# Hybrid decoder step on one core: a mixer stage with new weight slots, a packed step-size projection and a re-ordered chunk schedule

## What is computed

```python
proj = rmsnorm(x, g) @ w_in          # -> z 512 | xBC 1024 | dt 8 | q 512 | k 128 | v 128
xbc  = silu(causal_conv(xBC, width 4))
dt   = softplus(dt + dt_bias)        # step sizes, one per head
y_ssd = gated_norm(ssd_scan(xbc, dt, a, chunks of 128) + d_skip * x, z)   # 8 heads x 64, state 128
y_att = sliding_window_attention(q, k, v, window 128, sinks)              # 8 q heads, 2 kv heads
x = x + rmsnorm(concat(y_ssd, y_att) @ w_out)
mem_k, mem_v = rmsnorm(mem) @ w_xk, rmsnorm(mem) @ w_xv   # 256 rows, 1024 x 1024 each
... cross-attention into mem_k / mem_v, then a SwiGLU feed-forward
```

## Time and profile before

| what | value |
|---|---|
| median of 3 runs | 1830.93 us (1830.87 to 1839.26) |
| the profiled execution, its own time | 1835.19 us |
| its span, first to last instruction | 1833.5 us |
| busy share of the span: PE, weight loads, DVE, ACT, POOL | 91%, 86%, 49%, 41%, 12% |
| mean granted TensorE clock | 0.959 of 2.4 GHz |
| HBM traffic | 227.82 MB, 124 GB/s over the span |

### The profile page before, as it was taken

One profiled execution on the slowest core, in us unless ns is written; L12 is line 12 of the kernel. 1 busy time (PEld: TensorE's weight loads), 2 busy tenths in 40 slices (PEclk: granted clock), 3 DMA queues, 4 the chain that ended last, 5 costly groups with the idle time before them and its releaser, 6 DMA issues. The chain is left out here.

```text
span 1833.5 us, 27884 instructions
## 1 busy us (share of the span) xinstructions
PE 1675.7 (91%) x10764; PEld 1582.9 (86%) x10764; DVE 899.8 (49%) x1162; ACT 755.5 (41%) x1375; POOL 216.2 (12%) x317
## 2 busy tenths in 40 slices
PE   6999989778675998999999999999999999999996
PEld 6988777667654998999988999999999999999996
DVE  3466777766443365533444544443354443355443
ACT  3455655554333344443334433333233333344432
POOL 1012222222200012122222000000000000000000
PEclk9999999899975999999999999999999999999998
DMA  6542333222333854344353534454344453355651
GB/s 173 127 115 73 70 104 81 58 78 72 113 100 111 208 138 141 104 133 155 116 172 116 161 116 129 124 148 126 104 138 127 125 154 114 110 159 174 174 173 58
DMA packets 394147, 227.82 MB, mean 124 GB/s; under 512 B 33972, under 2 KB 384288, under 8 KB 394035
## 3 DMA queue, kind: packets, MB, share of 16 engines
q1 hardware_dynamic: 389442, 209.73, 40.1%
q0 software_dynamic: 4608, 16.78, 2.6%
HBM read 217.42 MB, written 10.07 MB: 124 GB/s over the span
## 5 line engine op out<-in xcount | busy, mean ns | idle before, releaser
L2547 DVE TENSOR_TENSOR ffn_lo<-ffn_raw,ffn_hi 128x1024 fp32r<-128x1024 f32 (+1 forms) x178 | 237.4, 1334 | 362.0 <-ACT ffn_hi L2475 362.0
L2614 PE MATMUL f_bank<-next_hi,ffn_hi 128*128 128x384 f32 (+1 forms) x1056 | 343.9, 326 | 10.1 <-DVE ffn_lo L2547 8.5
L2614 PE MATMUL f_bank<-next_lo,ffn_hi 128*128 128x384 f32 (+1 forms) x1056 | 343.0, 325 | 0.0
L2614 PE MATMUL f_bank<-next_hi,ffn_lo 128*128 128x384 f32 (+1 forms) x1056 | 342.7, 325 | 0.0
L2475 ACT ACTIVATE ffn_hi<-ffn_raw 128x1024 fp32r<-128x1024 f32 (+1 forms) x178 | 203.4, 1143 | 233.0 <-PE f_bank L2614 233.0
L2614 PEld LDWEIGHTS f_bank<-next_hi,ffn_hi 128*128 128x128 f32 x1056 | 200.2, 190 | 11.3 <-issue 9.2
L2614 PEld LDWEIGHTS f_bank<-next_hi,ffn_lo 128*128 128x128 f32 x1056 | 200.3, 190 | 0.0
L2614 PEld LDWEIGHTS f_bank<-next_lo,ffn_hi 128*128 128x128 f32 x1056 | 200.3, 190 | 0.0
L2614 PE MATMUL f_bank<-f_ahi,ffn_hi 128*128 128x384 f32 (+1 forms) x528 | 171.4, 325 | 0.2 <-DVE ffn_lo L2547 0.2
L2614 PE MATMUL f_bank<-f_ahi,ffn_lo 128*128 128x384 f32 (+1 forms) x528 | 170.8, 323 | 0.0
L2614 PE MATMUL f_bank<-f_alo,ffn_hi 128*128 128x384 f32 (+1 forms) x528 | 170.7, 323 | 0.0
(11 more groups left out here) (440 smaller groups left out, 3095.0 us busy)
## 6 DMA issues: line engine op xcount, KB each, us to landing
ffn_raw<-w_gate SPq DMA_DIRECT2D x66, 512.0 KB, 3.8
ffn_raw<-w_up SPq DMA_DIRECT2D x66, 512.0 KB, 3.7
ffn_raw<-w_down SPq DMA_DIRECT2D x48, 704.0 KB, 4.5
a_raw<-w_in SPq DMA_DIRECT2D x114, 256.0 KB, 3.3
b_raw<-w_xq SPq DMA_DIRECT2D x24, 512.0 KB, 4.0
b_raw<-w_xo SPq DMA_DIRECT2D x24, 512.0 KB, 4.1
xm<-x_prompt SPq DMA_DIRECT2D x16, 512.0 KB, 5.4
ffn_raw<-cache_mem_k POOLq DMA_DIRECT2D x16, 512.0 KB, 5.0
```

Of the source, the lines that this page charges most:

```text
L2547: dve.tensor_tensor(w_lo[:, s % 2, 0:kt], raw[:, s, 0:kt], w_hi[:, s % 2, 0:kt].bitcast(F32), ALU.subtract)\
L2614: ins = pe.matmul(out, a[:, s % 2, k, :], b[:, k0 + k, 0:w], start=(first and k == 0 and m == 0), stop=(last and k == kt - 1 and m == 2))
```

## The change

- The dt panel goes (`NPA` 19 to 18). Its 8 columns are loaded once, with the constants, split once, and put side by side as 64 stationary columns: hi in 0 to 7, lo in 32 to 39. A group's dt product is `dtm`, 16 matmuls (8 steps times hi and lo rows) into one bank; ACT copies it out, and `dtT` adds hi and lo while it transposes, through a stacked identity `both`.
- A memory panel is now 256 columns over half of the contraction. PE waits for one panel at a time, and a third slot for weights is found in the unused columns 256 to 383 of `h_hi`/`h_lo`.
- Steps move in the tables: `kq` to (0, 0), `cv0` to (0, 1) and (0, 3), the first tap to (1, 1), `yo` to (4, 1), `cvt` to (4, 2); DVE's part of `usq` becomes a step of its own, `un`, at (5, 3) behind the copy of the probabilities; `pv` and `uT` of the last half move to (0, 1) and (0, 2) of the next panel; the row transposes that stood ahead of a group move into its first panel.
- At the start PE makes all six transposes into six banks without waiting for their copies, and POOL, not DVE, makes the lo part of panel 0.

```diff
-NPA = NPT + 1
+NPA = NPT
...
-        later = c + 1 if c < 7 else None
-        at = {
-            (0, 0): [("pv", c - 1, 1)], (0, 1): [("uT", c - 1)], (0, 2): [("kq", c)],
-            (1, 0): [("sc", c, 0)], (1, 2): [("xT", c)], (1, 3): [("cb", c)],
-            (2, 0): [("seg", c)], (2, 1): [("den", c, 0)], (2, 3): [("zT", c)],
-            (3, 0): [("sc", c, 1)], (3, 1): [("pT", c, 0)], (3, 3): [("yd", c)],
-            (4, 0): [("yo", c)], (4, 1): [("cs", c)], (4, 2): [("pv", c, 0)], (4, 3): [("den", c, 1)],
-            (5, 0): [("usq", c)], (5, 2): [("pT", c, 1)],
-        conv = {(0, 0): [("cv0", later, 0)], (0, 1): [("cv0", later, 4)], (0, 3): [("tap", later, 1)], (1, 3): [("tap", later, 2)],
-                (3, 2): [("tap", later, 3)], (5, 0): [("cvt", later)], (5, 1): [("xc", later)], (5, 3): [("gates", later)]}
+        return {
+            (0, 0): [("kq", c)],
+            (1, 0): [("sc", c, 0)], (1, 2): [("xT", c)], (1, 3): [("cb", c)],
+            (2, 0): [("seg", c)], (2, 1): [("den", c, 0)], (2, 3): [("zT", c)],
+            (3, 0): [("sc", c, 1)], (3, 1): [("pT", c, 0)], (3, 3): [("yd", c)],
+            (4, 1): [("yo", c)], (4, 2): [("cs", c), ("den", c, 1)], (4, 3): [("pv", c, 0)],
+            (5, 0): [("usq", c)], (5, 2): [("pT", c, 1)], (5, 3): [("un", c)],
+        }
+        return {(0, 1): [("cv0", c, 0)], (0, 3): [("cv0", c, 4)], (1, 1): [("tap", c, 1)], (1, 3): [("tap", c, 2)],
+                (3, 2): [("tap", c, 3)], (4, 2): [("cvt", c)], (5, 1): [("xc", c)], (5, 3): [("gates", c)]}
+        return {(0, 1): [("pv", c, 1)], (0, 2): [("uT", c)]}
...
+    def new_rows(g):
+        t = halves(g)
+        if g == 3:
+            return {(0, 0): [("hT", *t[2]), ("hT", *t[3])]}
+        return {(0, 0): [("hT", *t[2]), ("hT", *t[3])], (0, 1): [("hT", *t[4]), ("hT", *t[5])]}
...
-    for m in range(6):
-        do["hT"](*halves(0)[m])
-    do["consts"]()
     for g in range(3):
-        do["panel"](NPA * g, lambda q: None)
...
-                extra = {(0, 3): [("dtT", g)], (1, 1): [("dt1", g)], (1, 3): [("dt2", g)], (2, 2): [("cum", g)]}
+                extra = {(0, 2): [("dtm", g)], (1, 0): [("dtT", g)], (1, 2): [("dt1", g)], (2, 0): [("dt2", g)], (2, 3): [("cum", g)]}
+                extra[5, 2] = [("hT", *x) for x in halves(g + 1)[0:2]]
+            at = join(left(c - 1) if c > 0 else {}, chunk(c) if c >= 0 else {}, conv(c + 1) if c >= -1 else {}, extra)
...
-            (0, 1): [("kq", c)], (1, 2): [("sc", c, 0)], (2, 0): [("xT", c), ("cb", c)], (2, 2): [("seg", c)], (3, 0): [("den", c, 0)],
-            (4, 0): [("zT", c), ("sc", c, 1), ("pT", c, 0)], (4, 2): [("yd", c)], (5, 2): [("yo", c)],
-            (6, 0): [("cs", c), ("pv", c, 0)], (6, 1): [("den", c, 1)], (6, 3): [("usq", c)], (7, 2): [("pT", c, 1)],
+            (0, 0): [("kq", c)], (0, 3): [("sc", c, 0)], (1, 1): [("xT", c)], (1, 2): [("cb", c)], (1, 3): [("seg", c)],
+            (2, 1): [("den", c, 0)], (2, 3): [("zT", c)], (3, 0): [("sc", c, 1)], (3, 1): [("pT", c, 0)], (3, 3): [("yd", c)],
+            (4, 2): [("yo", c)], (4, 3): [("cs", c), ("den", c, 1)], (5, 0): [("pv", c, 0)], (5, 2): [("usq", c)],
+            (6, 0): [("pT", c, 1)], (6, 3): [("un", c)], (7, 0): [("pv", c, 1)], (7, 2): [("uT", c)],
         }
-        if c == 7:
-            at = join({(0, 0): [("pv", 6, 1), ("uT", 6)]}, at)
-        else:
-            at = join(at, {(0, 2): [("cv0", 7, 0), ("cv0", 7, 4)], (1, 0): [("tap", 7, 1)], (3, 2): [("tap", 7, 2)], (5, 0): [("tap", 7, 3)],
-                           (6, 2): [("cvt", 7)], (7, 0): [("xc", 7)], (7, 3): [("gates", 7)]})
+        if c == 6:
+            at = join(new_rows(3), left(5), at,
+                      {(0, 2): [("cv0", 7, 0)], (1, 0): [("cv0", 7, 4)], (2, 0): [("tap", 7, 1)], (2, 2): [("tap", 7, 2)],
+                       (4, 1): [("tap", 7, 3)], (5, 3): [("cvt", 7)], (7, 1): [("xc", 7)], (7, 3): [("gates", 7)]})
-    do["pv"](7, 1)
-    do["uT"](7)
...
+        dtw = sc[:, 0, :].rearrange("p (k n) -> p k n", n=32)
...
+            (dtw[:, :, 0:HEADS], io["w_in"][:, C_DT:C_DT + HEADS].rearrange("(k p) n -> p k n", p=P)),
...
+                    w = io["w_xk" if n - MEM0 < KT else "w_xv"][512 * kh:512 * kh + 512, 256 * j:256 * j + 256]
                     for m in range(2):
-                        sp.dma_start(raw[:, n % 3, 4 * m:4 * m + 4], w[:, 4 * m:4 * m + 4]).then_inc(raw_full[n % 3], 16)
+                        sp.dma_start(raw[:, n % 3, 4 * m:4 * m + 4].rearrange("p (k a) n -> p k (a n)", a=2),
+                                     w[256 * m:256 * m + 256].rearrange("(k p) n -> p k n", p=P)).then_inc(raw_full[n % 3], 16)
...
+                        sp.wait_ge(consts_done, 14)
...
+                pool.wait_ge(S["hi_done"], ready(0))
+                pool.tensor_tensor(w_lo[:, 0], raw[:, 0], w_hi[:, 0].bitcast(F32), ALU.subtract).then_inc(S["lo_done"], 1)
...
-                act.wait_ge(S["panel_done"], ready(n - 2))
-                act.activation(w_hi[:, s2], raw[:, s3], ACT.Copy).then_inc(S["hi_done"], 1)
+                act.wait_ge(S["panel_done"], ready(n - 2 if n < MEM0 + 2 else MEM0 - 1 if n == MEM0 + 2 else n - 3))
+                act.activation(weights(w_hi, h_hi, n), raw[:, s3], ACT.Copy).then_inc(S["hi_done"], 1)
...
+                act.wait_ge(S["evac_done"], ready(NPA * g + T_V))
...
-                hi_ahead(n - 1)
-                hi_ahead(n)
+                if n == MEM0:
+                    hi_ahead(n + 2)
                 for q in range(4):
                     inner(q)
-                mem_evac(n)
+                if n % 2:
+                    for t in range(2):
+                        a, j = (n - MEM0) // KT, (n - MEM0) // 2 % 4
+                        act.wait_ge(*((S["panel_done"], ready(n)) if t else (S["t0_done"], ready((n - MEM0) // 2))))
+                        act.activation(mem_kv[:, a, t, 256 * j:256 * j + 256], bank[t][:, 0:256], ACT.Copy).then_inc(S["evac_done"], 1)
+                hi_ahead(n + 3)
+            def dtm(g):
+                act.wait_ge(S["dtT_done"], ready(2 * g))
+                act.activation(dtr[:, 0:GW[g]], bank[7][0:64, 0:GW[g]], ACT.Copy).then_inc(S["dtr_done"], 1)
...
+                hT(*halves(0)[0])
+                hi_ahead(0)
+                for m in range(1, 6):
+                    hT(*halves(0)[m])
+                hi_ahead(1)
...
-                lo_ahead(n)
+                lo_ahead(n + 2)
...
+                if n == MEM0:
+                    lo_ahead(n + 2)
-                if (n - MEM0) % 2:
-                    lo_ahead(n - 1)
-                    lo_ahead(n)
+                lo_ahead(n + 3)
...
-                    pe.wait_ge(S["hlo_done"], ready(HT_FIRST[g] + (2 if g else 5)))
+                    pe.wait_ge(S["hlo_done"], ready(HT_FIRST[g] + 2))
...
-                pe.wait_ge(S["hlo_done"], ready(m - 2))
+                if m >= 6:
+                    pe.wait_ge(S["hlo_done"], ready(m - 2))
...
-                pe.wait_ge(S["evac_done"], ready(NPA * g))
+                pe.wait_ge(S["dtr_done"], ready(g))
+                for u in range(n):
+                    mm_ = pe.matmul(bank[7][:, 8 * u:8 * u + 8], dtr[:, P * u:P * u + P], both[:], start=True, stop=True)
+                mm_.then_inc(S["dtT_done"], 1)
+            def dtm(g):
+                w = GW[g]
+                pe.wait_ge(S["dtw_lo"], ready(2))
+                for k in range(KT):
+                    for m, b in enumerate((h_hi, h_lo)):
+                        mm_ = pe.matmul(bank[7][0:64, 0:w], dtw_r[:, k, :], b[:, k, 0:w], start=(k == 0 and m == 0), stop=(k == KT - 1 and m == 1))
                 mm_.then_inc(S["dtT_done"], 1)
...
-                t = (n - MEM0) % 2
-                    pe.wait_ge(S["lo_done"], ready(n + 1))
-                    pe.wait_ge(S["evac_done"], ready(n - 1))
+                kh, n0 = n % 2, n - n % 2
+                pe.wait_ge(S["lo_done"], ready(n))
+                if n < MEM0 + 2:
+                    pe.wait_ge(S["hlo_done"], ready(HT_FIRST[3] + 1 + 2 * kh))
+                b_hi, b_lo = half_of(w_hi, h_hi, n), half_of(w_lo, h_lo, n)
+                for t in range(2):
+                    inner(2 * t)
+                    if kh == 0:
+                        pe.wait_ge(S["evac_done"], ready(n0 - 2 + t))
+                    for k in range(4):
+                        if k == 2:
+                            inner(2 * t + 1)
+                        for m, (a, b) in enumerate(((h_hi, b_hi), (h_hi, b_lo), (h_lo, b_hi))):
+                            mm_ = pe.matmul(bank[t][:, 0:2 * P], a[:, 4 * kh + k, P * t:P * t + P], b[:, k],
+                                            start=(kh == 0 and k == 0 and m == 0), stop=(kh == 1 and k == 3 and m == 2))
+                    if kh == 1 and t == 0:
+                        mm_.then_inc(S["t0_done"], 1)
+                mm_.then_inc(S["panel_done"], 1)
```

(38 more changed lines are left out.)

151 lines of the change are left out of this document (48 added, 103 removed).

## The result

The changed kernel takes 1807.4 us (median of 4 runs, 1804.97 to 1810.66) against 1831.2 for the kernel before (median of 4 runs): a ratio of 0.9856, 95% interval 0.9832 to 0.988. It is faster by 23.8 us. The profiled execution took 1804.97 us, its span 1803.2.

A forecast was written before the change was run, and what follows sets the result against it. PE's waits in 0 to 499 us, paid again in clock, were taken as the limit. Stage terms -3 - 2 - 8 - 14 - 19.2 = -46.2 us gave 1784 us; likeliest case 1772 to 1796 (0.64), range 1764 to 1810.

The forecast's parts named there:

- the third group's sum: Third group of rows: waits, clock and dt savings less the added waits, -14 us (bounds -6 and -20).
- Moving the first tap ... only takes DVE's wait for cv0 away from its head.: First tap step on DVE, moved from (0, 3) to (1, 1): only a wait at its head goes; no price.
- (c): Second half's `den` comes a quarter later and POOL needs 2.01 us: its waits may grow, 0 and +1.5 us.
- Clock: -5.2: Third group: the 9.7 us lost to the lower clock fall by about half, -5.2 us.
- (a): Second and third group: `dt2` stands later on DVE, so PE's `cum` wait grows, +3 us in each (0 to 4.7).
- (b): A group's last row transposes stand behind ACT's copies, PE waits mid first panel: +1.5 and +2.5 us (0 to 5).
- the sign of being wrong: PE's waits for lo parts appearing in the groups would show the prediction wrong, with DVE as bound; no size given.
- -16.3 for the lo parts: Memory panels: with three slots the splits hide behind two panels of PE, so the lo waits go, -16.3 us.
- VectorE becomes the bound: Rival: DVE's fixed order costs 3 us per chunk in both groups and 6 in the memory stage: 1808, chance 0.17.
- Slower: Rival: ACT stands at `kq` at each chunk's head until DVE passes `un`, delaying PE in 8 chunks: 1840, chance 0.05.
- The memory stage gained: Answers the rival that loads, not slots, hold the memory panels, so 19 us fall away: 1803, chance 0.05.
- far from all waits went: Answers the rival that nearly all PE waits in the three stages go: -68 us, 1763, chance 0.09.

The follow-up runs named there:

- e7: Changed kernel with each memory panel's weight split made two panels ahead instead of three, still halved by contraction and in three places: 1808.3 us.

## Why the prediction was right or wrong

The time, 1807.4, is in the range and on the side that was forecast, but at its end: of the 46.2 us of the sum 23.8 came, and the band of the likeliest case (1772 to 1796) was missed. The least that the bounds of the stages allow is 1 + 2 + 3 + 6 + 13 = 25 us, so the time lies just outside the sum itself; the range holds it because it was stretched for two rivals (1803 and 1808).

| stage | forecast (bounds) | measured |
|---|---|---|
| start | -3 (-1 to -4.2) | -4.0 |
| first group | -2 | -1.6 |
| second group | -8 (-3 to -14) | -4.9 |
| third group | -14 (-6 to -20) | **+2.2** |
| memory panels | -19.2 (-13 to -25) | -14.1 |

**The step that failed is the third group's sum** (-14 forecast; +2.2 measured, -1.5 in e7), in three of its terms.

- *"Moving the first tap ... only takes DVE's wait for cv0 away from its head."* It was priced at nothing. Before, the tap ran in time in which DVE had nothing to do; behind the scores it stands ahead of `den` of the first half. Putting it back gave 9.3 us. The `pT` waits grew by 5.0 (3.4 to 8.4). Term (c) was about the second half, and there it held: 0.9 to 1.9 us for its +1.5. The other 4.0 are the first half (2.5 to 6.5, in two waits of 3.5 and 3.0), for which the sum had no term. The tap is not the only cause: at chunk 4 it makes 1.3 us of the longer way to the reciprocal and the late hi split 3.7.
- *Clock: -5.2.* The stage's mean went from 0.93 to 0.91: 140.3 x 0.09 = 12.6 us lost instead of 9.7; in e7 it is 136.6 x 0.06 = 8.2. The step halved the loss because the longest waits went; as many us of waits came back, and the loss stayed about as it was. That a wait is paid a second time in clock holds only at times, as the two windows behind the wait of 3.5 us show.
- *What is late next.* The sum added 7 us for (a), (b) and (c). Named, the new waits are 2.6 (`cum`), 3.5 (rows, less the 0.4 of before), 5.0 (`pT`), 2.2 (`seg`) and 0.7 (lo): 14.0. (a) and (b) were of the right size, though the waits of (b) stand at the head of a group's first panel, not in its middle; `seg` was not seen, and the hi split behind ACT's copies was looked for as a wait of PE, when it is a wait of DVE that reaches PE by the scores.

**What held.** The `pv` waits went (6.5 to 1.3 us, 10.3 to 1.6, 2.3 to none) and in the groups so did the `qs` waits (beside the memory panels the scores now wait 1.7 us); undoing the order of `un` alone costs 18.1 us. The wait of `cum` with a drop of the clock behind it came as foretold (4.0 us), and lo waits in the groups, the sign of being wrong, are 0.9 us. Start: PE goes from its last transpose (16.94) into the first panel at 17.20, so the small dt load costs nothing. By the Trainium skill's rule on short descriptors ("DMA: Bandwidth & Descriptors", "Why small descriptors are slow (HBM only)") the prediction had estimated 2 us less gain; no wait of this trace shows them. dt: 16 matmuls of 384 columns start 0.176 us apart from 70.31 to 72.95, 2.8 us for the 4.16 of the earlier trace rows. In the second group the clock's loss fell by 2.9 us (5.7 to 137.7 x 0.02 = 2.8), 2.7 were forecast.

**Memory panels.** -16.3 for the lo parts was right to the last wait, but not by the third place, as the step had it (e7); what is left is the halving by contraction. Left out was ACT's copy of the finished panels, which PE now waits for because the next pair begins in the same banks: 7.6 us in 5 waits. `pT` in chunk 6 waits 0.9 and 0.7, not 3.

**The rivals.** "VectorE becomes the bound" gave the time (1808) and half the reason. The loss does run through DVE's fixed order; but DVE is not short of time: it idles 5.84 us at the head of chunk 4, and 19.6 us less work bought 1.2 us. "Slower", by the keys' wait on ACT, is there in small: ACT stands 2.23 us at the keys of chunk 4, and without that wait the time is 3.8 us less, which is not settled. The memory stage gained, and far from all waits went.

## What to carry to other kernels

When a step is moved in an in-order engine's program, price what it now stands in front of, also when the move is meant to help: a tap step of 2.4 us, moved out of idle time and ahead of a short chain to another engine, cost 9 us in the run that put it back. Look at what feeds the chain, too: at chunk 4 the larger part of the delay came from copies on ACT that stood ahead of the hi split. Waits that are removed one by one come back under the next name until the chain behind them is shorter, so add up the waits of a stage before and after, not those of one line. Five small steps of 0.9 us, ahead of the large ones instead of behind, came with 10.6 us less, of which the clock's part is unexplained: short links of a chain through several engines are worth trying first. And run the same code twice before reading a stage: one and the same third group took 140.3 and 136.6 us.

## What the runs showed of the hardware

Three things were not expected.

The first panel's matmuls (384 columns) start 0.32 us apart and later 0.17: before for 4.0 us (21.19 to 25.20), after for 2.1 us (17.20 to 19.29). The windows show a clock of 1.00 there, but that is no reading: the trace's first record of the clock begins at 25.5 us before and at 19.4 us after, where the spacing halves, and the view counts what lies ahead of it as full clock. The spacing ahead of the record, about twice the later one, fits the lower level. Before, PE had waited 2.63 us right ahead of the panel; after, it works without a pause from 13.33 us on. That is some 6 matmuls fewer at the slow spacing, 6 x 0.15 = 0.9 us of the first group's 1.6. The twelve kernels made from the kernel after share its start, and in them none to six matmuls are slow, with the first record between 16.1 and 19.3 us.

The same wait of 3.5 us is followed by the lower level in the kernel after and by the higher one in e7, with the same code.

Further, the untouched part of the program took 1326.6 to 1342.0 us in the fourteen profiles, its mean clock shown as 0.96 in each.

The Trainium skill, page "TensorE: Matmul & The Clock Gate", section "The HAM clock gate (the "warmup" mystery)", says that how many matmuls run slowly at a start differs between runs of one kernel. These rows agree. It also warns that the trace's records of the clock can't be fully trusted; here they begin where the spacing halves, and no row speaks against them.
